# A second retention head in block form: four token blocks summed during the first head's output product, kept in memory in two parts

## The reference, cut to what matters

```
proj = rmsnorm(x) @ w_in         # q, k, v, z_a, x_b, z_b, g_a, g_b, all from one projection
q, k = rope(q), rope(k) * 256 ** -0.5          # 4 retention heads, 256 columns of q and of k each
ret  = retention(q, k, v)                      # chunks with decay, and a recurrent state
o_a  = group_norm(ret) * silu(z_a)
o_b  = rglru(causal_conv(x_b)) * silu(z_b)
merged = sigmoid(g_a) * (o_a @ w_a) + sigmoid(g_b) * (o_b @ w_b)
x = x + merged @ w_o
```

## Time and profile before

| | before |
|---|---|
| median of 3 runs | 1887.71 us (1887.39 to 1889.06) |
| the profiled execution, its own time | 1886.3 us |
| its span | 1884.5 us |
| PE busy | 1862.4 us, 99% |
| DVE, ACT, POOL busy | 1379.8 us, 872.1 us, 325.2 us |
| granted clock of PE | 0.998 |
| transfers | 289.10 MB, 153 GB/s on average |

### The profile page before, as it was taken

The page is one execution under the profiler, slowest core; times in us unless marked ns, Lnnn a source line. Parts: engine busy times, 40 slices in busy tenths (PEclk is TensorE's granted clock), DMA queues, the critical chain, the costliest instruction groups (busy, mean ns, idle before and its releaser), DMA issues.

```text
span 1884.5 us, 32869 instructions
## 1 busy us (share of the span) xinstructions
PE 1862.4 (99%) x12908; PEld 1740.9 (92%) x12908; DVE 1379.8 (73%) x2338; ACT 872.1 (46%) x1440; POOL 325.2 (17%) x457
## 2 busy tenths in 40 slices
PE   8999999999999999999999999999999999999998
PEld 7899898897899999999998988988989999999997
DVE  7777677676766877866797776867867678878575
ACT  5432344433437776543444323434433377766334
POOL 2221130130231210100122211303102422001010
PEclk9999999999999999999999999999999999999999
DMA  6436565484443333643655455754844533327353
GB/s 221 138 126 211 181 212 161 159 262 140 146 152 92 104 99 99 155 134 103 201 175 160 146 176 176 235 162 151 283 125 134 167 101 105 101 87 185 96 163 113
DMA packets 131479, 289.10 MB, mean 153 GB/s; under 512 B 13790, under 2 KB 54222, under 8 KB 131198
## 3 DMA queue, kind: packets, MB, share of 16 engines
q1 hardware_dynamic: 93710, 166.23, 28.4%
q0 software_dynamic: 37472, 120.78, 20.9%
q10 hardware_dynamic: 144, 0.00, 0.0%
HBM read 223.29 MB, written 53.97 MB: 147 GB/s over the span
## 4 chain that ended last, share of the span: by engine, by line
PE 82%; DVE 7%; DMA 4%; ACT 3%; DVEq 2%; issue 1%; ACTq 1%; SPq 0%
PE bank L2668 17%; PE bank L2670 16%; PE bank L2669 16%; PE bank L2762 4%; PE bank L2764 4%; PE bank L2763 4%; DMA w_raw<-in_w_units 3%; PE bank L2779 3%; PE bank L2782 3%; PE bank L2781 3%; PE sums L2838 2%; PE sums L2762 1%; PE sums L2764 1%; PE sums L2763 1%; DVE w_lo L732 1%
## 5 line engine op out<-in xcount | busy, mean ns | idle before, releaser
L2668 PE MATMUL bank<-xn_hi,w_hi 128*128 128x296 f32 (+1 forms) x1760 | 527.3, 300 | 1.6 <-DVE acc L2596 0.6
L2670 PE MATMUL bank<-xn_lo,w_hi 128*128 128x296 f32 (+1 forms) x1760 | 522.7, 297 | 0.0
L2669 PE MATMUL bank<-xn_hi,w_lo 128*128 128x296 f32 (+1 forms) x1760 | 522.1, 297 | 0.0
L2668 PEld LDWEIGHTS bank<-xn_hi,w_hi 128*128 128x128 f32 x1760 | 330.9, 188 | 8.7 <-issue 6.1
L2669 PEld LDWEIGHTS bank<-xn_hi,w_lo 128*128 128x128 f32 x1760 | 331.3, 188 | 0.9
L2670 PEld LDWEIGHTS bank<-xn_lo,w_hi 128*128 128x128 f32 x1760 | 330.6, 188 | 0.0
L732 DVE TENSOR_TENSOR w_lo<-w_raw,w_hi 128x1024 fp32r<-128x1024 f32 x203 | 248.9, 1229 | 69.9 <-ACT w_hi L722 64.8
L722 ACT ACTIVATE w_hi<-w_raw 128x1024 fp32r<-128x1024 f32 x203 | 212.4, 1054 | 181.6 <-DMA w_raw<-in_w_units 178.3
L2668 PE MATMUL bank<-oa_hi,w_hi 128*128 128x296 f32 (+1 forms) x512 | 153.7, 300 | 0.0
L2669 PE MATMUL bank<-oa_hi,w_lo 128*128 128x296 f32 (+1 forms) x512 | 151.9, 297 | 0.0
L2670 PE MATMUL bank<-oa_lo,w_hi 128*128 128x296 f32 (+1 forms) x512 | 151.7, 296 | 0.0
(11 more groups left out here) (376 smaller groups left out, 4264.3 us busy)
## 6 DMA issues: line engine op xcount, KB each, us to landing
w_raw<-in_w_units SPq DMA_DIRECT2D x173, 512.0 KB, 3.7
w_raw<-in_w_units SPq DMA_DIRECT2D x199, 256.0 KB, 4.0
S<-in_state_ret POOLq DMA_DIRECT2D x64, 512.0 KB, 5.2
out_ret_s<-S POOLq DMA_DIRECT2D x64, 512.0 KB, 6.2
sum_raw<-sum_scr POOLq DMA_DIRECT2D x16, 592.0 KB, 11.1
w_raw<-in_w_units POOLq DMA_DIRECT2D x32, 256.0 KB, 4.7
sum_scr<-sum_raw POOLq DMA_DIRECT2D x8, 592.0 KB, 4.7
vst<-v_scr SPq DMA_DIRECT2D x8, 512.0 KB, 3.8
```

The source lines that it names most:

```text
L2668: pe.matmul(ps, w_hi[:, slot, cols], x_hi, start=first, stop=False)
L2669: pe.matmul(ps, w_lo[:, slot, cols], x_hi, start=False, stop=False)
L2670: return pe.matmul(ps, w_hi[:, slot, cols], x_lo, start=False, stop=last)
```

## The change

Head 1 joins the block form, so the four token sums have to be there before its first products. What is done where:

- **DVE** no longer adds the tokens' two parts, and no longer empties the banks of head 0's output product. It makes the four combinations and the four low parts in that stage, once per layer.
- **ACT** copies the high part of four token quarters into four planes (`high_tokens`), empties head 0's 16 output jobs (`first_taken`) and makes the four high parts once per layer (`high_sum`).
- **POOL** adds the low parts of the quarters onto the four planes by adding transfers (`add_tokens`, 592 KB each, SBUF to SBUF). In head 1 it stores eight planes (high and low) in place of four, and ahead of heads 2 and 3 it loads eight in place of four; nothing is split again there. The loads of four states at the start of heads 1, 2 and 3 now wait for the queries' A11.
- **DVE** and **ACT** get a wait for all eight stores in head 1 before they write `ktok` and `vtok`.
- In the block heads ACT's `keep_sum(queries, S2)` goes ahead of `part_high(queries, A22)`, and DVE's `split_lo(1)` and the freeing of a bank go ahead of `turned(2)`.

```diff
-PAIR_HEADS = (2, 3)
+PAIR_HEADS = (1, 2, 3)
@@ POOL
+                def add_tokens():
+                    for n, (to, k, half) in enumerate(TOKENS):
+                        a, b = HALVES[half]
+                        pool.wait_ge(right_hi, l * HIGHS + n + 1)
+                        pool.dma_start(sum_raw[:, to, :, :], xn_lo[:, k:k + 4, a:b].bitcast(f32), accum_op=ADD)\
+                            .then_inc(again_in[n], 16)
+
                 def store_sums():
-                    for n, plane in enumerate((DIFF, EDGE, MIX2, LAST)):
-                        pool.wait_ge(right_ready, l * READIES + n + 1)
+                    for n in (LAST, EDGE, DIFF, MIX2):
+                        pool.wait_ge(right_lo, l * RIGHTS + n + 1)
...
+                        for plane in (SUMS + n, n):
+                            pool.dma_start(sum_scr[plane], sum_lohi[:, plane, :, :].rearrange("p k t -> p (k t)").bitcast(f32))\
+                                .then_inc(sums_out, 16)
...
                     if h in PAIR_HEADS:
                         add_part(head_pairs(h)[1], S3)
+                        if h == PAIR_HEADS[0]:
+                            store_sums()
+                        pool.wait_ge(part_done, PART_AT[l] + head_pairs(h)[1] * PRODUCTS + A11 + 1)
                     for n in range(S_RING):
                         load_state(n)
...
                     if h + 1 in PAIR_HEADS:
-                        load_sums(h)
+                        if h + 1 == PAIR_HEADS[0]:
+                            add_tokens()
+                        else:
+                            load_sums(h)
@@ ACT, block heads
+                        keep_sum(queries, S2, bank[queries % 2], 2, HALF)
                         part_high(queries, A22)
-                        keep_sum(queries, S2, bank[queries % 2], 2, HALF)
@@ ACT, end of a head
+                    split_hi(act, "R", l, h, 11)
+                    if h + 1 == PAIR_HEADS[0]:
+                        keys = head_pairs(h + 1)[0]
+                        high_tokens(0)
+                        high_tokens(1)
...
+                        first_taken(0, 0)
+                        high_tokens(2)
+                        high_tokens(3)
+                        first_taken(0, 1)
+                        split_hi(act, "R", l, h, 12)
+                        first_taken(1, 0)
+                        high_sum(DIFF)
+                        first_taken(1, 1)
+                        split_hi(act, "R", l, h, 13)
+                        high_sum(MIX2)
+                        first_taken(2, 0)
+                        high_sum(EDGE)
+                        part_high(keys, A11)
+                        first_taken(2, 1)
+                        high_sum(LAST)
+                        part_high(keys, S1)
+                        first_taken(3, 0)
...
@@ DVE
-                        step = {(0, 0): 2, (0, 1): 3, (1, 0): 4, (2, 0): 5, (2, 1): 6, (3, 0): 7}.get((i, n))
-                        if step:
-                            token_sum(step)
...
+                        if i == 4 and h == PAIR_HEADS[0]:
+                            dve.wait_ge(sums_out, (l + 1) * SUMS_OUT)
@@ DVE, end of a head
+                    if h + 1 == PAIR_HEADS[0]:
+                        grow_four(0)
+                        split_lo(dve, "R", l, h, 12)
+                        token_sum(DIFF)
+                        token_sum(MIX2)
+                        token_sum(EDGE)
+                        sum_low(DIFF)
+                        split_lo(dve, "R", l, h, 13)
+                        token_sum(LAST)
+                        sum_low(MIX2)
+                        grow_four(1)
+                        first_parts()
+                        sum_low(EDGE)
+                        split_lo(dve, "R", l, h, 14)
+                        second_parts()
+                        split_lo(dve, "R", l, h, 15)
@@ PE, block_pair
+                        elif two < 2:
+                            pe.wait_ge(right_lo, l * RIGHTS + n)
+                        else:
+                            pe.wait_ge(again_in[n - 1], l * AGAIN + 16 + two // 2 * 32)
```

More of the change, by code:

```diff
@@ L503, in trunk @@
         sum_lohi = alias("sum_lohi", R["vo"][0], [P, 2 * SUMS, 4, HALF], f32r)
-        assert R["vo"][0] + 6 * 4 * HALF * 4 <= R["ktok"][0] and R["vo"][0] + 8 * 4 * HALF * 4 <= R["kst"][0]
-        DIFF, MIX2, EDGE, LAST, RAW12, RAW22 = range(6)
+        assert R["vo"][0] + 2 * SUMS * 4 * HALF * 4 <= R["kst"][0]
+        DIFF, MIX2, EDGE, LAST = range(SUMS)
+        RAW12, RAW22 = SUMS + EDGE, SUMS + LAST
+        TOKENS = ((RAW12, 0, 1), (DIFF, 0, 0), (RAW22, 4, 1), (LAST, 4, 0))
         turn_snap = alias("turn_snap", R["S"][0] + S_RING * 2 * DV * 4, [P, 3, HALF])
@@ L1311, in _, with high_tokens @@
                             act.drain().then_inc(sp_ready, 1)
-                    for i in range(11, 16):
-                        split_hi(act, "R", l, h, i)
-                    if h + 1 in PAIR_HEADS:
-                        for plane in (DIFF, MIX2, EDGE, LAST):
-                            act.wait_ge(again_in[plane], l * AGAIN + 16 * (PAIR_HEADS.index(h + 1) + 1))
-                            act.activation(sum_lohi[:, SUMS + plane, :, :], sum_raw[:, plane, :, :], ACT.Copy)\
-                               .then_inc(right_hi, 1)
-                        for part in (A11, S1, S2, A12):
-                            part_high(head_pairs(h + 1)[0], part)
+                    def high_tokens(n):
+                        to, k, half = TOKENS[n]
+                        a, b = HALVES[half]
+                        act.activation(sum_raw[:, to, :, :], xn_hi[:, k:k + 4, a:b].bitcast(f32), ACT.Copy)\
+                           .then_inc(right_hi, 1)
@@ new lines, in _ @@
+                    split_hi(act, "R", l, h, 11)
[3 more added lines that the diff above has]
+                        high_tokens(1)
+                        if l >= 1:
+                            act.wait_ge(x_stored, l * 16)
+                        first_taken(0, 0)
[15 more added lines that the diff above has]
+                        first_taken(3, 0)
+                        split_hi(act, "R", l, h, 14)
+                        part_high(keys, S2)
+                        first_taken(3, 1)
+                        split_hi(act, "R", l, h, 15)
+                        part_high(keys, A12)
+                    else:
+                        for i in range(12, 16):
+                            split_hi(act, "R", l, h, i)
+                        if h + 1 in PAIR_HEADS:
+                            for part in (A11, S1, S2, A12):
+                                part_high(head_pairs(h + 1)[0], part)
@@ L2784, in product, with block_pair @@
                     ins.then_inc(part_done, 1)
-                def block_pair(two, columns, right, lows, jobs, nth):
+                def block_pair(two, columns, right, jobs, nth):
                     (a0, b0), (a1, b1) = columns
```

173 lines of the change are left out of this document (84 added, 89 removed).

## The result

The changed kernel takes 1943.15 us (median of 4 runs, 1941.55 to 1944.27), the kernel before beside it 1888.13 us. The ratio is 1.029, with a 95% interval of 1.0277 to 1.0302: slower by 2.9%, 55 us, where 1890 was forecast and 1903 was the end of the range.

A forecast was written before the change was run, and what follows sets the result against it. PE, busy 99% of the span, was taken as the bound. Terms -4.0 - 2.5 + 0 + 8.7 = +2.2 us on 1886.3 give 1888.5; with the median 1.4 above, 1890, range 1880 to 1903.

The forecast's parts named there:

- the doubled stores of head 1: Head 1's eight stores, 4.85 MB, 16 us, starting after its keys' S3: taken to cost 0.
- the cover: Rest of the pairs and first values in head 1, 15 to 20 us until DVE comes to `ktok`, hiding the stores.
- PE waits at `keys` or `values` of head 1, behind the eight stores: Sign in the changed kernel's profile that the forecast is wrong; no size or chance given.
- The chain in the output product: Head 0's output product: token copies, adds and splits finish late, delaying PE 4.2 and 4.5 us by layer, together +8.7.
- case B: Head 0's output product: adds priced by packet, 6.5 us each, total 1909; at 5 us an add 1897; chance 0.17.
- Rival C: Heads 2 and 3: doubled loads make S1 late, DVE holds banks, +2 to +3 us a head, total 1900; chance 0.08.
- The 5.4 us of which DVE was relieved: Heads 2 and 3: low parts DVE no longer makes, letting it catch up, so the eight loads were taken as 0.
- The saved products: Head 1's q and k in block form: -2.3 us in layer 0, -1.7 in layer 1, together -4.0.
- Heads 2 and 3 relieved: Splits gone and orders changed: head 3 of layer 0 gains 2.2 us, the three others 0.1 each, together -2.5.

The follow-up runs named there:

- c6: Changed kernel with DVE token sums, earlier `grow_four(1)`, one plane per sum in memory, four stores or adds after the first value unit, each add awaiting its own plane: 1884.89 us.
- e3: The changed kernel with only the two planes that `ktok` overwrites stored early, the other six after head 1's first value unit: 1917.15 us.
- c1: The changed kernel with DVE adding the token quarters itself and six of the eight stores after the first value unit: 1912.34 us.
- c5: c1 with `grow_four(1)` moved earlier, the eight loads in their old order: 1896.58 us, ratio 1.0047 to the kernel before.
- e2: The changed kernel with head 1's four state loads waiting until PE is through with the first value unit: 1928.39 us.
- e4: The changed kernel with value units laid out in memory to come in rows of 2 KB instead of 512 bytes: 1926.76 us.
- b1: The kernel before with only the three changes of order (`keep_sum`, state loads, `split_lo` 1), heads 2 and 3 only: 1883.98 us, ratio 0.9981.

## Why the prediction was wrong, point by point

The steps from the changed kernel to c6 make a ladder, each step taken from the run before it: the stores -26.0 (e3, 1943.15 to 1917.15), the token sums by DVE -4.8 (c1, to 1912.34), the earlier `grow_four(1)` -15.8 (c5, to 1896.58), one plane per sum -11.7 (c6, to 1884.89), which leaves 3.0 us of gain by c6's ratio. In another order the shares differ: with the token sums first they are worth 14.4 and the stores 16.4. The forecast had, in the same order, 0, +8.7 for the two of the chain, 0, and -6.5. The -4.8 is a difference of two single runs and the softest of the steps.

- **The step that failed is "the doubled stores of head 1 ... I take 0".** The bytes and the start were right (4.85 MB, behind S3). What was looked at is the wrong waiter: the cover was counted up to `ktok` on DVE, while SP's first value unit is asked for in the same stretch, and the states' loads stand behind the stores and fill the engines too, although nobody needs the states soon. The prediction listed "PE waits at `keys` or `values` of head 1, behind the eight stores" as a sign of being wrong, but gave it no rival, no price and no chance; it is what came. 4.85 + 2.1 MB at the 355 MB per ms that POOL's queue reached (7.21 MB in 78% of 26 us) are 19.6 us of all engines, so the queue that starts at 166.3 is full until past 186 even if it had them alone; the unit is wanted at 182.9. Measured in place of 0: 20.9 us of wait, with 5 more for the clock behind it, and -26.0 when the stores are moved (e3). e2, e3 and e4 each take most of the wait away by another side (14, 21, 16 us of it): states, stores, short rows, with the unit asked for at the same time within 1 us.
- **The chain in the output product** was the right mechanism, mis-sized: +8.7 forecast, 20.6 on the ladder (4.8 and 15.8). Not all of the 15.8 is this chain's: with `grow_four(1)` the plane stores and state loads behind it on POOL go out earlier too. S3 was to land at 155.9 and reached ACT at 163.36, 7.5 us later. Of that 1.4 is the later first add and 2.3 the three adds at 4.8 us instead of 4.05, near case B's 5 us an add. The largest piece, 3.8, is S3's own way: 5.4 us after issue was taken from a row in which S3 went out 3 us after the state stores; here it goes out right behind them and takes 9.2. That the stores in front are the reason fits the four kernels above (5.4, 6.5, 8.3, 9.2) but was not tested by moving S3 alone.
- **Rival C happened**, with a chance of 0.08. The eight loads make S1 late and DVE stands before it with the bank copies behind it, 5.07 us in the row above, PE 1.8 to 2.8 us a head, the forecast +2 to +3. c5 against c6 gives its price, 11.7 us: by the stretches 9.7 less in the output products of heads 1 and 2 and 5.7 less in the q and k behind them, against 3.8 more in head 1, where c6's own stores and adds lie. The 5.4 us of which DVE was relieved were no help: a wait for a transfer is not shortened by an engine that has time.
- **The saved products** (-4.0) were right in place and size: in c6 head 1's q and k take 24.44 and 23.89 us, -1.6 and -1.9. But nearly all of it goes back in the values behind them, which had no gap before: their first 196 matmuls take 39.92 and 37.89 us, for 37.36 and 37.18 in b1, +2.6 and +0.7, with waits for `vtok_lo` and for a load from `v_scr` beside the adding transfers.
- **Heads 2 and 3 relieved** (-2.5) was right in size and place (head 3 of layer 0): b1 shows -3.6, and it needs only the orders, not the kept parts. The splits taken off ACT and DVE showed no worth: c6 does them all again, and its q and k of heads 2 and 3 (23.23 to 23.79 us) are as fast as b1's (23.20 to 24.29). In the changed kernel itself the relief was hidden: its head 3 of layer 0 still waits 1.1 us for `turn_snap`, where the prediction saw no such wait.
- The sum: 26.0 for the stores, 20.6 for the chain, 11.7 for the loads, less 3.0, is 55.3 us, for 55.0 measured. That it closes is no proof, since each step starts where the last one ends; the stretches of the changed kernel, read against the earlier trace rows above, give 55 without the ladder.

So the best version with head 1 in the block form, c6, equals the reordered kernel before: 0.9984 (0.9975 to 0.9994) and 0.9981 (0.9972 to 0.9990). What the block form of head 1 brings beyond the orders can be read from the traces: from the start of head 0's output product to the start of head 1's, c6 takes 132.46 and 128.84 us in the two layers, b1 131.57 and 130.09. That is 0.4 us less of one execution each, 3.5 gained at q and k and 3.3 given back in the values: no gain that could be told from none. The 9.6 us that `grow_four(1)` brings in layer 1 are in c1 3.6 us of wait for S3, 3.0 for the value unit, and 2.9 of slower matmuls at a clock of 0.90; open is which of the transfers on POOL's list makes the value unit late there.

## What to carry to other kernels

A kept result that is doubled in memory (high and low part) costs twice the transfers, at the store and at each reload, and saves splits only; ask first whether the splits were on the path. Cost a burst of stores by the queues of others that share the engines: list every transfer asked for until the burst has drained, not only the reader of the freed buffer. And take a transfer's time from issue to landing only together with what was issued in front of it in that row of the trace.

## What the runs showed of the hardware

- Adding transfers from on-chip memory to on-chip memory, in rows of 1184 bytes, fill the engines here. From 126 to 142 us of the changed kernel, the queues:

```profile
q0 software_dynamic: 1934, 2.51, 90.2%
q1 hardware_dynamic: 705, 1.28, 24.0%
```

  That is 2.51 MB in 14.4 us of all engines, 174 MB per ms, half of the 355 that the queue reached with the plane stores and state loads. Most of the 2.51 MB are the four adds (2.42 MB in full); part adds of 256 KB and the end of `ret_p`'s store lie in the window too. The figure of the Trainium skill that the prediction weighed (page "DMA: Bandwidth & Descriptors", section "Anatomy of one DMA — SWDGE (gpsimd) path": bytes at 436 GB/s) does not hold for them.
- From 166 to 192 us SP's queue, beside POOL's full one, moved 1.60 MB in 22.1% of the engines' time with value units in rows of 512 bytes, and 2.22 MB in 22.8% with rows of 2 KB (e4).
- PE's granted clock was 1.00, its higher level (2.4 GHz), through all stretches of c6 above. In the 11.4 us without work of the changed kernel it was 0.60 and from 194.29 to 200.00, with PE busy again, 0.59, most of the time its lower level (1.2 GHz); from 200 on it was 1.00. So the stretch behind the wait took 31.03 us without a gap instead of 28.88. A wait of 11.2 us cost 2.2 more in this way, one of 9.7 in layer 1 cost 2.8 more.
- The six transfers of 592 KB of c6's head 1, four of them adding onto memory off the chip, took 10.6 us in the median from issue to landing, beside SP's loads.
